# Up projections of a two-block network: high and low halves of the rows side by side in one matmul, and the bank's two halves summed by ScalarE and VectorE

## The chip, the cores and the metric

The kernel runs on one core of one Trainium2 chip. The time is that of the device, from the start of the program to its end, in microseconds (us); smaller is better. A core has a matmul engine (TensorE, PE in the profile, with its weight loads as PEld), three engines for everything else (VectorE or DVE, ScalarE or ACT, GpSimd or POOL) and a queue for loads (SyncE, SP). Each runs its own program in order, and they wait for one another by semaphores. Matmuls write to PSUM, eight banks of 128 x 512 fp32.

## What is computed

Two blocks of two layers each, on 256 rows of 1024 features. The first block has attention and a feed-forward part with a causal convolution over the rows; the second block is not touched by the change. Its part that matters here, cut:

```python
D_MODEL, SEQ, DEPTH, CONV_WIDTH = 1024, 256, 2, 3
D_FF = 2816                      # 22 tiles of 128

def conv_ffn(h, w_up, conv_w, conv_b, w_down):
    u = causal_dwconv(h @ w_up, conv_w, conv_b)   # 1024 -> 5632, three taps along the rows
    g, up = jnp.split(u, 2, axis=-1)
    return (jax.nn.silu(g) * up) @ w_down         # 2816 -> 1024

# in first_block, for both layers:
    x = x + conv_ffn(rms_norm(x, ln_ffn_g[i]), w_up[i], conv_w[i], conv_b[i], w_down[i])
```

## The kernel before

**Halves.** A matmul takes both operands in a reduced fp32 form. To keep precision each operand is split in two, a high half (the value rounded to that form) and a low half (the rest), and each product is the sum of three matmuls: high x high, high x low, low x high. Weights come by DMA as units of 128 x 1024 fp32 (512 KB) into RAW, five slots. `split` makes the high half SPH on ScalarE (L1437) and the low half SPL on VectorE (L1985), four slots; a slot is used again when TensorE has done with the unit four before it. So the halves of a unit are made at most four units ahead. The activations' halves are HTH and HTL, laid out as 8 tiles of the contraction (kt) by 512 columns; the feed-forward part uses columns 0 to 255, the 256 rows.

**The feed-forward stage.** `block1` runs it for layer 0 and 1, here FFN 0 and FFN 1. For each of 22 tiles j, TensorE does the up unit of side 0 (the gate) and of side 1, then the down unit of tile j - 2. An up unit is `turned` on half a bank: for each kt three matmuls of 256 columns (L975 high x high, L976 with the rows' low half, L977 with the weights' low half), 24 in all. Both sides of a tile share one bank, side 0 in columns 0 to 255 and side 1 in the rest. A down unit is 12 matmuls of 512 columns (L1139 to L1141) into banks 4 to 7. In FFN 0 the up banks are 0, 1 and 2; in FFN 1 they are 0 to 3.

**What follows an up tile (`up`).** When both sides are in the bank, ScalarE makes FC for both sides (L1557: last tap and bias), VectorE adds the two other taps to each side, reading the bank (L2198, L2201, twice), ScalarE takes the tanh (L1561), VectorE finishes the gated product FT (L2206, L2210), ScalarE rounds it to AH (L1568), and GpSimd subtracts to get AL (L2604). AH and AL are what the down unit needs. I call VectorE's first L2198 of a tile "the start of FC on VectorE". The bank is free after VectorE's last L2201.

**Order.** There is no scheduler at run time. `Schedule` writes one list of steps, and each engine's program takes its own share of it in that order. Whenever a weight unit is asked for (`get_w`), the splits of the next units are written into the list just there. In a tile the list reads: up of j, split, (down unit of j - 2), split, up unit of side 0 of j + 1, split, up unit of side 1, up of j + 1. Into FFN 0 are woven, in tiles 1 to 18, the matmuls of another projection (`ada`, L1040), whose weights aren't split; in tile 3 ScalarE also issues four table loads. FFN 1 has in tile 2 the norm statistics of the second block's context, in tile 3 the rope tables, in tiles 5 to 12 one context product each (`prod`: two small matmuls, VectorE, ScalarE, and VectorE or GpSimd).

## Time and profile before

| | us |
|---|---|
| median of three runs (2135.65 to 2137.37) | 2136.27 |
| span of the profiled execution | 2132.1 |
| TensorE busy in it | 2081.3 |
| VectorE busy | 1337.3 |
| ScalarE busy | 961.3 |
| GpSimd busy | 134.3 |

The profile is of one execution and its span leaves out what lies around the program, 4.2 us against the median. FFN 0 lies from about 154 to 354 us, FFN 1 from about 499 to 693. A busy time is the sum of an engine's instructions; matmuls overlap, each is listed with 0.28 or 0.39 us, while the next starts 0.12 or 0.23 us after it. So distances are read from start to start. In the timelines a row is a start, a length, the engine and the line, and at its end, where there is one, how long the engine was idle before it and who ended that.

### The profile page before, as it was taken

What the parts mean: (1) busy time and instruction counts of PE and PEld (TensorE: products, weight loads), DVE (VectorE), ACT (ScalarE), POOL (GpSimd) and SP (SyncE); (2) the same over time, 40 slices, a digit from 0 to 9 for tenths busy, and PEclk for the clock granted to TensorE, in tenths of its full rate; (3) what the DMA queues carried; (4) which work ended last, traced back from release to release, by engine and by line L of the source; (5) the groups of instructions that cost most, each with busy time, mean ns of one, the idle gap of its engine ahead of it and who ended that gap; (6) DMA issues with size and microseconds to landing.
All of it is one profiled execution on the core that took longest, in us unless ns stands there. A gap on an engine that the chain in (4) does not pass through costs nothing.

```text
span 2132.1 us, 31611 instructions
## 1 busy us (share of the span) xinstructions
PE 2081.3 (98%) x12202; PEld 1795.3 (84%) x12202; DVE 1337.3 (63%) x2333; ACT 961.3 (45%) x1602; POOL 134.3 (6%) x140
## 2 busy tenths in 40 slices
PE   8999999999999999999999999999989999999998
PEld 6779998778999888888888788888877899888997
DVE  6756667667777227548445556868563578475665
ACT  4545555554555425353333453232343554445443
POOL 1001000000110100000100001111110000100100
PEclk9999999999999999999999999999999999999999
DMA  8436655534555321222222104534224234251553
GB/s 258 144 129 239 227 209 193 162 100 166 181 178 176 126 99 60 70 70 70 79 89 89 60 30 152 197 109 158 100 100 141 89 126 140 91 178 55 193 169 129
DMA packets 79099, 284.23 MB, mean 133 GB/s; under 512 B 8790, under 2 KB 9698, under 8 KB 78952
## 3 DMA queue, kind: packets, MB, share of 16 engines
q1 hardware_dynamic: 70848, 256.15, 35.5%
q10 hardware_dynamic: 6072, 18.73, 2.4%
q0 software_dynamic: 2032, 7.35, 1.2%
q8 instruction: 98, 1.61, 0.3%
q14 instruction: 49, 0.40, 0.1%
HBM read 276.35 MB, written 5.83 MB: 132 GB/s over the span
## 4 chain that ended last, share of the span: by engine, by line
PE 80%; DVE 10%; ACT 6%; issue 2%; DMA 2%; POOL 0%; DVEq 0%; ACTq 0%; SPq 0%
PE pb L975 15%; PE pb L977 15%; PE pb L976 15%; PE pb L988 5%; PE pb L990 5%; PE pb L989 5%; DVE SPL L1985 3%; PE pb L994 2%; PE pb L1139 2%; ACT SPH L1437 2%; PE pb L1141 2%; PE pb L1140 2%; PE pb L1316 2%; PE pb L1213 2%; PE pb L1297 2%
## 5 line engine op out<-in xcount | busy, mean ns | idle before, releaser
L1985 DVE TENSOR_TENSOR SPL<-RAW,SPH 128x1024 fp32r<-128x1024 f32 x462 | 561.0, 1229 | 409.3 <-ACT SPH L1437 395.7
L975 PE MATMUL pb<-HTH,SPH 128*128 128x256 f32 (+1 forms) x2008 | 646.6, 322 | 6.8 <-DVE HTL L2063 3.0
L977 PE MATMUL pb<-HTH,SPL 128*128 128x256 f32 (+1 forms) x2008 | 637.4, 317 | 0.0
L976 PE MATMUL pb<-HTL,SPH 128*128 128x256 f32 (+1 forms) x2008 | 637.2, 317 | 0.0
L1437 ACT ACTIVATE SPH<-RAW 128x1024 fp32r<-128x1024 f32 x462 | 476.8, 1048 | 243.0 <-PE pb L977 118.9
L975 PEld LDWEIGHTS pb<-HTH,SPH 128*128 128x128 f32 x2008 | 382.2, 190 | 38.3 <-issue 4.7
L976 PEld LDWEIGHTS pb<-HTL,SPH 128*128 128x128 f32 x2008 | 382.4, 190 | 26.2
L977 PEld LDWEIGHTS pb<-HTH,SPL 128*128 128x128 f32 x2008 | 382.2, 190 | 26.0
L988 PE MATMUL pb<-SPH,HTH 128*128 128x512 f32 x640 | 254.9, 398 | 2.5 <-ACT GV L1635 2.0
L990 PE MATMUL pb<-SPL,HTH 128*128 128x512 f32 x640 | 250.6, 392 | 0.0
L989 PE MATMUL pb<-SPH,HTL 128*128 128x512 f32 x640 | 250.2, 391 | 0.0
L988 PEld LDWEIGHTS pb<-SPH,HTH 128*128 128x128 f32 x640 | 120.9, 189 | 29.7 <-issue 2.7
L990 PEld LDWEIGHTS pb<-SPL,HTH 128*128 128x128 f32 x640 | 120.6, 188 | 25.9
L989 PEld LDWEIGHTS pb<-SPH,HTL 128*128 128x128 f32 x640 | 121.1, 189 | 23.8
L975 PE MATMUL pb<-ABH,SPH 128*128 128x512 f32 (+1 forms) x384 | 131.6, 343 | 1.7 <-DVE SPL L1985 1.1
L977 PE MATMUL pb<-ABH,SPL 128*128 128x512 f32 (+1 forms) x384 | 129.8, 338 | 0.0
L976 PE MATMUL pb<-ABL,SPH 128*128 128x512 f32 (+1 forms) x384 | 129.8, 338 | 0.0
L975 PEld LDWEIGHTS pb<-ABH,SPH 128*128 128x128 f32 x384 | 72.3, 188 | 10.7 <-issue 2.2
L1798 ACT ACTIVATE GT<-pb,BG 128x512 f32<-128x512 f32 (+1 forms) x48 | 27.8, 579 | 117.9 <-PE pb L977 117.9
L977 PEld LDWEIGHTS pb<-ABH,SPL 128*128 128x128 f32 x384 | 72.2, 188 | 8.6
L976 PEld LDWEIGHTS pb<-ABL,SPH 128*128 128x128 f32 x384 | 72.3, 188 | 8.5 <-issue 0.2
L1139 PE MATMUL pb<-SPH,AH 128*128 128x512 f32 x176 | 71.3, 405 | 1.8 <-ACT SPH L1437 1.8
(274 smaller groups left out, 2503.3 us busy)
## 6 DMA issues: line engine op xcount, KB each, us to landing
RAW<-in_w_up SPq DMA_DIRECT2D x88, 512.0 KB, 4.5
RAW<-in_wa SPq DMA_DIRECT2D x64, 512.0 KB, 3.3
RAW<-in_w_in SPq DMA_DIRECT2D x48, 512.0 KB, 4.6
...
```

The costliest lines, as they stand in the source:

```text
L975: T.matmul(o, wh[:, kt, :], xh[:, kt, n0:n1], start=kt == 0, stop=False)
L976: T.matmul(o, wh[:, kt, :], xl[:, kt, n0:n1], start=False, stop=False)
L977: m = T.matmul(o, wl[:, kt, :], xh[:, kt, n0:n1], start=False, stop=kt == 7)
L988: T.matmul(P[:, :], xh[:, kt, c], wh[:, j, :], start=kt == 0, stop=False)
L989: T.matmul(P[:, :], xl[:, kt, c], wh[:, j, :], start=False, stop=False)
L990: m = T.matmul(P[:, :], xh[:, kt, c], wl[:, j, :], start=False, stop=kt == 7)
L994: return T.transpose(o, i, ident)
L1139: T.matmul(P[:, :], xh, wh, start=j == 0, stop=False)
L1140: T.matmul(P[:, :], xl, wh, start=False, stop=False)
L1141: m = T.matmul(P[:, :], xh, wl, start=False, stop=end)
L1437: A.activation(hi, raw, ACT.Copy, scale=1.0).then_inc(*act.tick(s["hi"], ("u", u)))
L1985: W.tensor_tensor(lo, raw, hi.bitcast(F32), SUB).then_inc(*dve.tick(s["lo_dve"], ("u", u)))
```

## The change

Each side of an up tile gets a bank of its own. HTH and HTL become the two parts of one array HT2, so that one matmul can stream the 256 rows' high halves and their low halves, 512 columns, past the weights' high half. The new function `paired` does this: for each kt one matmul of 512 columns over the whole bank and one of 256 with the weights' low half into the first half of the bank; for the last kt the order is reversed. The bank's first half then holds two of the three products, its second half the third. A new step `up_sum` follows each up unit: ScalarE copies the second half to the new array FU, VectorE adds the first half to it and frees the bank. `up` then reads FU and no longer the bank; ScalarE's FC of a side now waits for VectorE's sum of that side.

```diff
         for j in range(FF_TILES + 2):
             if j < FF_TILES:
-                n = self.take(LO4 if l else (0, 1, 2), ("up", l, j))
                 for side in range(2):
                     u = self.get_w(f"w_up{l}", side * FF_TILES + j)
+                    n = self.take(LO4 if l else (0, 1, 2), ("up", l, j, side))
                     self.add("up_mm", l, j, side, u)
                     self.put_w(u)
+                    self.add("up_sum", l, j, side)
+                    self.give(n)
                 self.add("up", l, j)
-                self.give(n)
...
+    def paired(P, hi, lo, src, kts=range(8)):
+
+        wh, wl = (a.rearrange("p (k c) -> p k c", k=8) for a in (hi, lo))
+        both = sb["AB2" if src[0] == "AB" and src[2] != "s" else "HT2"]
+        apart = P[:, :].rearrange("p (a n) -> p a n", a=2)
+        for kt in kts:
+            rows(src, kt)
+            xs = both[:, :, kt, 0:256]
+            if kt < 7:
+                T.matmul(apart, wh[:, kt, :], xs, start=kt == 0, stop=False)
+            m = T.matmul(apart[:, 0, :], wl[:, kt, :], both[:, 0, kt, 0:256], start=False, stop=False)
+            if kt == 7:
+                m = T.matmul(apart, wh[:, kt, :], xs, start=False, stop=True)
+        return m
...
     def up_mm(l, j, side, u):
-        P = bank(("up", l, j))
-        hi, lo = halves(u)
-        m = turned(P[:, side * 256:side * 256 + 256], hi, lo, (f"f{l}",), 0, 256)
+        P = bank(("up", l, j, side))
+        m = paired(P, *halves(u), (f"f{l}",))
...
+    def up_sum(l, j, side):
+        name = ("up", l, j, side)
+        act.wait_ge(mm, name)
...
+        A.activation(sb["FU"][:, j % 2, side, :], k.P(name)[:, 256:512], ACT.Copy, scale=1.0).then_inc(
+            *act.tick(s["ffn_act"], ("low", l, j, side)))
+
     def up(l, j):
-        P, C, i = k.P(("up", l, j)), sb["FC"], j % 2
+        C, i = sb["FC"], j % 2
         for side in range(2):
             ft = side * FF_TILES + j
-            act.wait_ge(mm, ("up", l, j, 1))
+            act.wait_ge(*k.read(("up", l, j, side)))
...
-            A.activation(C[:, i, side, :], P[:, side * 256:side * 256 + 256], ACT.Identity,
+            A.activation(C[:, i, side, :], sb["FU"][:, i, side, :], ACT.Identity,
...
+    def up_sum(l, j, side):
+        name, U = ("up", l, j, side), sb["FU"][:, j % 2, side, :]
+        dve.wait_ge(s["ffn_act"], ("low", l, j, side))
+        W.tensor_tensor(U, k.P(name)[:, 0:256], U, ADD).then_inc(*dve.free(*k.read(name)))
+
...
-            c, u = C[:, i, side, :], P[:, side * 256:(side + 1) * 256]
+            c, u = C[:, i, side, :], sb["FU"][:, i, side, :]
             dve.wait_ge(s["ffn_act"], ("c", l, j, 1))
```

What this does to the order, on VectorE in FFN 0, from the start of FC of tile 20 to that of tile 21. L1985 is a weight split; pb0 is the bank. Before:

```order
L2198 SCALAR_TENSOR_TENSOR FC_132<-pb0,PAR_55,FC_132 128x255 [waits ffn_act]
L2201 SCALAR_TENSOR_TENSOR FC_132<-pb0,PAR_55,FC_132 128x254 [waits ffn_dve]
L2198 SCALAR_TENSOR_TENSOR FC_132<-pb0,PAR_55,FC_132 128x255
L2201 SCALAR_TENSOR_TENSOR FC_132<-pb0,PAR_55,FC_132 128x254 [waits ffn_dve]
L2206 SCALAR_TENSOR_TENSOR FT_133<-FT_133,FC_132 128x256 [waits ffn_act]
L2210 SCALAR_TENSOR_TENSOR FT_133<-FT_133,FC_132 128x256 [waits read0,ffn_dve]
L1985 TENSOR_TENSOR SPL_51<-RAW_49,SPH_50 128x1024 [waits mm,hi,raw1]
L1985 TENSOR_TENSOR SPL_51<-RAW_49,SPH_50 128x1024 [waits mm,hi,raw2]
L1985 TENSOR_TENSOR SPL_51<-RAW_49,SPH_50 128x1024 [waits mm,hi,raw3]
L2198 SCALAR_TENSOR_TENSOR FC_132<-pb1,PAR_55,FC_132 128x255 [waits ffn_act]
```

The same place after; L2011 is the split, L2220 the sum, L2229 and L2232 the two taps:

```order
L2229 SCALAR_TENSOR_TENSOR FC_130<-FU_132,PAR_54,FC_130 128x255 [waits ffn_act]
L2232 SCALAR_TENSOR_TENSOR FC_130<-FU_132,PAR_54,FC_130 128x254 [waits ffn_dve]
L2229 SCALAR_TENSOR_TENSOR FC_130<-FU_132,PAR_54,FC_130 128x255
L2232 SCALAR_TENSOR_TENSOR FC_130<-FU_132,PAR_54,FC_130 128x254 [waits ffn_dve]
L2236 SCALAR_TENSOR_TENSOR FT_131<-FT_131,FC_130 128x256 [waits ffn_act]
L2240 SCALAR_TENSOR_TENSOR FT_131<-FT_131,FC_130 128x256 [waits ffn_dve]
L2011 TENSOR_TENSOR SPL_51<-RAW_49,SPH_50 128x1024 [waits mm,hi,raw1]
L2011 TENSOR_TENSOR SPL_51<-RAW_49,SPH_50 128x1024 [waits mm,hi,raw2]
L2220 TENSOR_TENSOR FU_132<-pb1,FU_132 128x256 [waits ffn_act]
L2011 TENSOR_TENSOR SPL_51<-RAW_49,SPH_50 128x1024 [waits mm,hi,raw3]
L2220 TENSOR_TENSOR FU_132<-pb2,FU_132 128x256 [waits ffn_act]
L2229 SCALAR_TENSOR_TENSOR FC_130<-FU_132,PAR_54,FC_130 128x255 [waits ffn_act]
```

A sum stands between the second and the third split, and another between the third split and FC. On ScalarE, from FC of tile 20 to that of tile 21, before (L1557 FC, L1437 the high half of a split):

```order
L1557 ACTIVATE FC_132<-pb0,PAR_55 128x256 [waits ffn_pool,ffn_act,mm]
L1557 ACTIVATE FC_132<-pb0,PAR_55 128x256
L1561 ACTIVATE FT_133<-FC_132 128x256 [waits ffn_dve]
L1568 ACTIVATE AH_134<-FT_133 128x256 [waits ffn_dve]
L1437 ACTIVATE SPH_50<-RAW_49 128x1024 [waits raw1]
L1437 ACTIVATE SPH_50<-RAW_49 128x1024 [waits mm,raw2]
L1437 ACTIVATE SPH_50<-RAW_49 128x1024 [waits mm,raw3]
L1557 ACTIVATE FC_132<-pb1,PAR_55 128x256 [waits ffn_pool,ffn_act,mm]
```

And after (L1569 is the copy of up_sum, L1583 FC, L1452 the high half); `read0` to `read2` are the signals that VectorE's sum gives when it frees that bank:

```order
L1583 ACTIVATE FC_130<-FU_132,PAR_54 128x256 [waits ffn_pool,ffn_act,read2]
L1583 ACTIVATE FC_130<-FU_132,PAR_54 128x256 [waits read0]
L1587 ACTIVATE FT_131<-FC_130 128x256 [waits ffn_dve]
L1594 ACTIVATE AH_133<-FT_131 128x256 [waits ffn_dve]
L1452 ACTIVATE SPH_50<-RAW_49 128x1024 [waits raw1]
L1452 ACTIVATE SPH_50<-RAW_49 128x1024 [waits mm,raw2]
L1569 ACTIVATE FU_132<-pb1 128x256 [waits ffn_act,mm]
L1452 ACTIVATE SPH_50<-RAW_49 128x1024 [waits raw3]
L1569 ACTIVATE FU_132<-pb2 128x256 [waits ffn_act,mm]
L1583 ACTIVATE FC_130<-FU_132,PAR_54 128x256 [waits ffn_pool,ffn_act,read1]
L1583 ACTIVATE FC_130<-FU_132,PAR_54 128x256 [waits read2]
```

FC waited for TensorE (`mm`) and now waits for a bank that VectorE frees (`read`); a copy stands ahead of the third high half, and one behind it. The pattern is the same in each tile.

## Rows read from the trace of the kernel before

**Rows 1.** The page's first section: busy time, share and instructions of each engine.
```profile
PE 2081.3 (98%) x12202; PEld 1795.3 (84%) x12202; DVE 1337.3 (63%) x2333; ACT 961.3 (45%) x1602; POOL 134.3 (6%) x140
```
**Rows 2.** Busy time by stretch, FFN 1; then granted clock, DMA share, GB/s.
```profile
core 0: us, PE busy (x) PEld busy (x) DVE busy (x) ACT busy (x) POOL busy (x), PEclk, DMA share, GB/s
640.00:680.00 40.00, 40.00 (x280) 37.42 (x280) 29.11 (x44) 20.88 (x33) 2.97 (x4) 1.00 0.60 197
```
**Rows 3.** TensorE's waits, 150 to 355 us, then 500 to 700: total, times, longest.
```profile
PE pb L975 <- DVE HTL L2063: 1.4, 1, 1.4
...
PE pb L1139 <- ACT SPH L1437: 1.8, 1, 1.8
```
**Rows 4.** VectorE's timeline in FFN 0: start, length, engine, line, idle time before.
```profile
337.90 0.48 DVE L2198 SCALAR_TENSOR_TENSOR FC<-pb,PAR,FC 128x255 f32<-128x255 f32 x1 [0.84 <-ACT FC L1557]
...
342.09 3.50 DVE L1985 TENSOR_TENSOR SPL<-RAW,SPH 128x1024 fp32r<-128x1024 f32 x3 [1.49 <-ACT SPH L1437]
346.43 0.48 DVE L2198 SCALAR_TENSOR_TENSOR FC<-pb,PAR,FC 128x255 f32<-128x255 f32 x1 [0.84 <-ACT FC L1557]
```
**Rows 5.** ScalarE's timeline, same place.
```profile
336.84 1.02 ACT L1557 ACTIVATE FC<-pb,PAR 128x256 f32<-128x256 f32 x2 [1.47 <-PE pb L977]
...
340.95 2.94 ACT L1437 ACTIVATE SPH<-RAW 128x1024 fp32r<-128x1024 f32 x3
```
**Rows 6.** VectorE's timeline, first tiles of FFN 1: the starts of FC.
```profile
506.47 0.48 DVE L2198 SCALAR_TENSOR_TENSOR FC<-pb,PAR,FC 128x255 f32<-128x255 f32 x1 [1.49 <-ACT FC L1557]
...
512.94 0.48 DVE L2198 SCALAR_TENSOR_TENSOR FC<-pb,PAR,FC 128x255 f32<-128x255 f32 x1
...
519.40 0.48 DVE L2198 SCALAR_TENSOR_TENSOR FC<-pb,PAR,FC 128x255 f32<-128x255 f32 x1
...
529.27 0.47 DVE L2198 SCALAR_TENSOR_TENSOR FC<-pb,PAR,FC 128x255 f32<-128x255 f32 x1
...
537.85 0.47 DVE L2198 SCALAR_TENSOR_TENSOR FC<-pb,PAR,FC 128x255 f32<-128x255 f32 x1
...
545.62 0.48 DVE L2198 SCALAR_TENSOR_TENSOR FC<-pb,PAR,FC 128x255 f32<-128x255 f32 x1
```
**Rows 7.** TensorE's timeline: up and down units in FFN 0; then wide matmuls elsewhere.
```profile
330.89 0.28 PE L975 MATMUL pb<-HTH,SPH 128*128 128x256 f32 x1
...
336.64 0.39 PE L1139 MATMUL pb<-SPH,AH 128*128 128x512 f32 x1
...
339.42 0.28 PE L975 MATMUL pb<-HTH,SPH 128*128 128x256 f32 x1
...
17.00 0.39 PE L989 MATMUL pb<-SPH,HTL 128*128 128x512 f32 x1
...
22.01 0.39 PE L990 MATMUL pb<-SPL,HTH 128*128 128x512 f32 x1
```
**Rows 8.** Groups by form: count, busy us, mean ns of one, idle before.
```profile
L1557 ACT ACTIVATE FC<-pb,PAR 128x256 f32<-128x256 f32 x88 | 44.8, 559 | 50.5 <-PE pb L977 50.5
...
L2429 DVE SCALAR_TENSOR_TENSOR GT<-GT,pb 128x256 f32<-128x256 f32 x16 | 6.7, 419 | 1.0
...
L1746 ACT ACTIVATE WA<-WA,PAR 128x256 f32<-128x256 f32 x8 | 4.1, 507 | 17.5 <-DVE WA L2332 17.5
```
**Rows 9.** VectorE's timeline in FFN 1: a tile with a context product, and the last tile.
```profile
554.59 0.48 DVE L2198 SCALAR_TENSOR_TENSOR FC<-pb,PAR,FC 128x255 f32<-128x255 f32 x1 [0.82 <-ACT FC L1557]
...
559.25 3.50 DVE L1985 TENSOR_TENSOR SPL<-RAW,SPH 128x1024 fp32r<-128x1024 f32 x3 [1.50 <-ACT SPH L1437]
...
685.62 0.48 DVE L2198 SCALAR_TENSOR_TENSOR FC<-pb,PAR,FC 128x255 f32<-128x255 f32 x1 [0.84 <-ACT FC L1557]
```
**Rows 10.** VectorE's timeline in FFN 0: the first tile, and the one with table loads.
```profile
161.03 0.48 DVE L2198 SCALAR_TENSOR_TENSOR FC<-pb,PAR,FC 128x255 f32<-128x255 f32 x1 [1.50 <-ACT FC L1557]
...
182.78 0.48 DVE L2198 SCALAR_TENSOR_TENSOR FC<-pb,PAR,FC 128x255 f32<-128x255 f32 x1
...
188.71 3.50 DVE L1985 TENSOR_TENSOR SPL<-RAW,SPH 128x1024 fp32r<-128x1024 f32 x3 [3.24 <-ACT SPH L1437]
```

More of the change, by code:

```diff
@@ L2713, in build @@
     o = m.put("SPL", o, [128, 4, 1024], F32R)
[L2714 to L2715 removed]
+    o = m.put("HT2", o, [128, 2, 8, 512], F32R)
     D = o
```

27 lines of the change are left out of this document (15 added, 12 removed).

## The prediction

> **What bounds the kernel now.** I read the page's first section, then busy time by stage, then the waits of TensorE, and last the timelines of the three engines around one FFN tile. TensorE is busy for 2081.3 of 2132.1 us [rows 1]. In the stretch of FFN 1 it is busy all of the time, VectorE 29.11 of 40 us and ScalarE 20.88 of 40, at granted clock 1.00 [rows 2]. Once an FFN stage is under way TensorE waits 1.8 us in FFN 1 and 1.4 us in FFN 0, once each [rows 3]. So TensorE sets the time, and the other two look as if they had a quarter or half to give. The busy share hides something, though: they form a ring. Per FFN tile (one j: two up units, one down unit) VectorE does three weight splits and six small steps, ScalarE does its share between them, and each waits for the other in program order. Take the tile whose FC work starts on VectorE at 337.90. ScalarE can't make the next high half before AH is done, at 340.95; VectorE can't make the low half before 342.09, which is 4.19 us after 337.90. Three low halves follow at (3.50 - 1.23) / 2 = 1.135 us from start to start, 3.41 us; then VectorE is idle 0.84 us until ScalarE's FC, which waited for TensorE, and starts again at 346.43 [rows 4, 5]. **The ring is 4.19 + 3.41 = 7.60 us long; TensorE's tile is 346.43 - 337.90 = 8.53 us.** That ring is real where TensorE leaves it alone: with two low halves it should be 4.19 + 2 x 1.135 = 6.46, and the starts 506.47, 512.94 and 519.40 lie 6.47 apart, the last two with no idle time before them [rows 6].
>
> **Part 1, the matmuls.** Each up unit has 24 matmuls of 256 columns; it gets 8 of 512 and 8 of 256. The columns streamed are the same, 6144. In [rows 7] 48 narrow starts take 336.64 - 330.89 = 5.75 us, 0.1198 each. Twelve wide ones take 339.42 - 336.64 = 2.78 us, 0.2317 each; elsewhere 22 wide starts take 22.01 - 17.00 = 5.01 us, 0.2277. So a merged pair saves between 0.2396 - 0.2317 = 0.008 and 0.2396 - 0.2277 = 0.012 us, eight pairs a unit, 88 units: 5.6 to 8.4 us in the kernel. I take 0.16 us a tile, 7.0 us, where TensorE stays the bound. The wide moving operand is now two blocks of 256, 16 KB apart; no row shows that form. The bounds are a gain of 8.4 and, if a wide one cost two narrow starts, none; a loss is rival C. I take the middle of the rows, since addresses are the only thing new.
>
> The Trainium skill ("TensorE: Matmul & The Clock Gate", section "Back-to-back issue gap") gives the spacing of a warm matmul as N/2.4 + 2.5 ns, 215.8 ns for 512 columns and 109.2 for 256. By that a pair would save 2.6 ns and the kernel 1.8 us; this trace has 228 to 232 and 120 ns, so the rows are used [rows 7].
>
> **Part 2, the sums.** Each up unit gets a ScalarE copy of the bank's second half (up_sum), then a VectorE addition that frees the bank. ScalarE's FC step moves behind the addition of its side. The order rows in the section on the change show where: VectorE now runs low half, low half, sum of side 0, low half, sum of side 1, FC. A 256-wide VectorE step with a bank among its inputs is 0.419 us [rows 8]. What this does to the ring, step by step:
> - Sum 0 stands between low halves: 0.42, less the 1.23 - 1.135 = 0.09 by which independent steps overlap, 0.33 us. Its ScalarE copy can start about 5 us after FC, after two high halves, while VectorE reaches the sum only at 4.19 + 2 x 1.135 = 6.46; the copy is hidden, and so is the one of side 1.
> - Sum 1 is followed by ScalarE's FC of side 1, which needs its result: 0.42 + 0.04. The 0.04 is the hand-over seen from ScalarE's FC end, 336.84 + 1.02 = 337.86, to VectorE's start at 337.90 [rows 4, 5].
> - That FC step used to lie beside VectorE's low halves, since it needed TensorE alone. Now it is in the ring: 0.56 + 0.04. The row with the bank as input has 0.559; its nearest SBUF-only kin, with a scale, has 0.507 [rows 8]. FC of side 0 is done meanwhile.
> Together 0.33 + 0.46 + 0.60 = **1.39 us, so the ring becomes 9.0 us against TensorE's 8.53 - 0.16 = 8.37.** VectorE falls 0.6 us behind a tile. It can do so only until its low halves come late: the low half made right after FC (342.09 + 1.23 = 343.3) is for the down unit that TensorE starts at 339.42 + 5.75 = 345.2 [rows 4, 7], so 1.9 us of cover, of which the later FC start takes about 0.5. The two short tiles at the start (part 3) alone use that up. From then on TensorE waits for a low half in every tile and the stage runs at the ring's pace. The matmul saving is then worth nothing there.
>
> Bounds of the 1.39: with FC at 0.507, 1.34; with nothing overlapped at sum 0 and a sum at FC's 0.48 us [rows 4], 0.42 + 0.06 + 0.06 more, 1.55. No row excludes a slightly shorter sum, so I allow 1.30; a ring shorter than before is excluded, since two steps and a wait come into it and none goes.
>
> **Part 3, FFN 1 by tiles.** Starts of FC before: 506.47, 512.94, 519.40, 529.27, 537.85, 545.62 [rows 6]; eight tiles with context products at 554.59 - 545.62 = 8.97; eight plain ones at 8.53; the last FC is at 685.62 [rows 9]. In all 179.15 us for 21 steps. After:
> - two steps with two splits, ring-bound before: 2 x (6.47 + 1.39) = 15.7
> - the step with the context statistics and the one with the rope tables, ring-bound before (9.87 and 8.58): + 1.39 each, 21.2
> - one plain step, 9.0
> - eight with a product: there VectorE's low half starts 559.25 - 554.59 = 4.66 after FC, not 4.19 [rows 9], so 9.46 each, 75.7
> - eight plain, 72.0
> Sum 193.6, which is **+14.5 us**.
>
> **Part 4, FFN 0.** 161.03 to 346.43 [rows 10, 4] is 185.4 us for 21 steps. Here TensorE also runs ada matmuls, so its tile is longer: from 182.78 to 346.43, 18 steps, 9.09 us on average, and 8.93 with the saving. The ring of 9.0 is about the same. After: two short steps 15.7; one plain 9.0; the step with the table loads, where VectorE's first low half comes 188.71 - 182.78 = 5.93 after FC [rows 10], 9.0 + 1.74 = 10.7; seventeen at 9.0, 153.0, and three more ScalarE row copies of 0.3 between them, 0.9. Sum 189.3, **+3.9 us**. The start and the end of the stages I count at nothing: the first FC comes some 0.3 later in each, the last tile's tail some 0.5 shorter, since TensorE's queue there is shorter. The three-bank ring of FFN 0 (a bank a side now, three sides deep, not three tiles) doesn't bind: sum 0 frees its bank 6.5 us after FC, TensorE wants it again after a down unit and an up unit more.
>
> **The sum.** 14.5 + 3.9 = +18.4 us on the profiled 2132.1 us. The median of the runs is 2136.3, 4.2 more for what lies around the span, which doesn't change. Forecast **2154.7 us**, 0.9% slower. About 42 steps scale with the 1.39: at 1.30 it is 3.8 us less, at 1.55 6.7 more, so 2151 to 2161; the count of steps in which TensorE is really held adds a few us either way, mostly in FFN 0, 2147 to 2165.
>
> **Rivals.**
> A, faster: the sums fit in VectorE's free time and TensorE stays the bound. For it: 27% of VectorE's time is free in [rows 2], and TensorE hardly waits now [rows 3]. It needs the three additions to stay under 8.37 - 7.60 = 0.77 us. Two 0.42 sums alone pass that, before the FC hand-over. It would give 2136.3 - 7.0 = 2129.3.
> B, no difference: the ring grows by about 1.0, to 8.6. This would happen if FC of side 1 were hidden by something I misread in the order. FFN 1 would lose 21 x (8.6 - 8.37) plus the start, some +7, FFN 0 would gain 3: about 2140.
> C, slower than forecast: a merged matmul of two blocks runs at its listed 0.39 us and not at 0.23. Then TensorE's tile is 8.37 + 16 x 0.16 = 10.9 us and becomes the bound again, 42 steps 2.2 us longer each: about 2228. From this rival's point on, 0.27 us a wide matmul, TensorE is slower than the ring. Against it: each matmul of the trace starts long before the one ahead ends, at every width [rows 7].
> D, the clock. I expect TensorE idle for 1.8 + 2 x 1.39 = 4.6 us in one piece, in FFN 1 behind the context statistics, where it waits 1.8 now [rows 3]. The granted clock is 1.00 in the stretch of rows 2, and no row here shows the other level. Should one down unit of 2.78 us behind the gap take twice as long, that is 2.8 us more, of which the ring, setting the pace, may take back some: about 2157.
> The same page of the Trainium skill (section "HAM oscillation — how this bites in real kernels") warns that idle gaps between bursts of matmuls return the clock to half rate; no row here shows it, and it gives D its place.
> E, the merging isn't one: each wide matmul is split again. The ring doesn't ask TensorE, so FFN 1 stays as it is and FFN 0 loses about 1: 2156.
>
> **Chances.** Forecast 0.74, A 0.10, B 0.06, C 0.03, D 0.05, E 0.02. A measurement of this kernel can tell about 0.2% (4.3 us) from no change. A is faster. B is around the edge, 4 in 6 counted as the same. The forecast's low tail, if FFN 0 gains and the ring is short, is the rest of "same". The range goes from 2146 to 2166, which holds the forecast, D, E, and leaves A, B and C out. Faster 0.10, same 0.05, slower 0.85.
>
> **What would show it.** Right: VectorE's FC starts 9.0 us apart in plain tiles of FFN 1 and 9.4 to 9.5 with a product; no idle time on VectorE between the sum of side 1 and FC other than ScalarE's FC, some 0.6; TensorE waiting for a low half (the split's line) at the down units, 0.6 us a tile, some 20 us in FFN 1; TensorE's busy time lower by some 7 us or more. Outside the two FFN stages every distance as before. Wrong: FC starts at 8.37 (A), TensorE waiting on a bank rather than a low half, wide matmuls starting over 0.24 us apart (C), or a granted clock under 1.00 (D).

## The result: 1.1% slower, by the ring of VectorE and ScalarE

| | before | after |
|---|---|---|
| median of the runs, us | 2135.96 (four, 2135.1 to 2137.37) | 2161.76 (four, 2158.15 to 2164.5) |
| ratio, with 95% interval | | 1.0113 (1.0102 to 1.0125) |
| span of the profiled execution | 2132.1 | 2156.3 |
| FFN 0, first to last FC start | 185.4 | 190.2 |
| from there to the first FC start of FFN 1 | 160.0 | 165.3 |
| FFN 1, first to last FC start | 179.1 | 194.6 |

The changed kernel takes 25.8 us more by the medians and 24.2 by the spans; the forecast was 18.4 more, 2154.7 us, range 2146 to 2166. The two stages are what was forecast (+4.8 for +3.9, +15.4 for +14.5). The rest lies between them, where I had counted nothing. In the spans 24.2 - 18.4 = 5.8 us are missing from the forecast: 1.8 in the stages, 5.3 between them, 0.2 ahead of the first FC, and 1.6 the other way behind the last one. The medians miss by 7.1; the other 1.3 is that after's profiled execution lies further under its kernel's median than before's. (A run's time is some 1.8 us over its span in nearly all runs that list both, so of the 4.2 put down to "what lies around the program" more than half is that this one profiled execution was short.)

The busy line of the profile after, which answers to [rows 1]:

```profile
PE 2087.4 (97%) x11498; PEld 1760.9 (82%) x11498; DVE 1367.9 (63%) x2421; ACT 992.1 (46%) x1690; POOL 135.3 (6%) x140
```

There are 704 matmuls fewer, yet TensorE is busy for 6 us more. A busy time counts a matmul ahead of a wait with its whole length, 0.39 us where the next one used to start after 0.23, and 42 such waits would make some 7 us; matmuls at half clock are listed longer still, with 0.63 us. This is an estimate, no run sets the parts apart. VectorE still looks idle for more than a third of the time and ScalarE for more than half. The stretch of [rows 2] after; at the end of a row stand granted clock, DMA share and GB/s:

```profile
640.00:680.00 40.00, 38.44 (x200) 31.95 (x199) 29.37 (x50) 24.17 (x40) 3.70 (x5) 1.00 0.52 173
```

TensorE is no longer busy all of the time, although its clock is full. VectorE's timeline of after, a plain tile in FFN 1 from FC to FC (L2229 FC, L2011 the low half, L2220 the sum; columns as in [rows 4]):

```profile
693.27 0.48 DVE L2229 SCALAR_TENSOR_TENSOR FC<-FU,PAR,FC 128x255 f32<-128x255 f32 x1 [0.67 <-ACT FC L1583]
...
697.48 2.36 DVE L2011 TENSOR_TENSOR SPL<-RAW,SPH 128x1024 fp32r<-128x1024 f32 x2 [1.49 <-ACT SPH L1452]
699.75 0.42 DVE L2220 TENSOR_TENSOR FU<-pb,FU 128x256 f32<-128x256 f32 x1
700.09 1.22 DVE L2011 TENSOR_TENSOR SPL<-RAW,SPH 128x1024 fp32r<-128x1024 f32 x1
701.22 0.42 DVE L2220 TENSOR_TENSOR FU<-pb,FU 128x256 f32<-128x256 f32 x1
702.31 0.48 DVE L2229 SCALAR_TENSOR_TENSOR FC<-FU,PAR,FC 128x255 f32<-128x255 f32 x1 [0.67 <-ACT FC L1583]
```

702.31 - 693.27 = 9.04 us, forecast 9.0. Nothing in that ring waits for TensorE any more: the two idle times are for ScalarE, 1.49 for the high half and 0.67 for FC of side 1, which is the step that had lain beside other work. ScalarE, same place:

```profile
700.21 0.60 ACT L1583 ACTIVATE FC<-FU,PAR 128x256 f32<-128x256 f32 x1 [0.38 <-DVE FU L2220]
701.67 0.60 ACT L1583 ACTIVATE FC<-FU,PAR 128x256 f32<-128x256 f32 x1 [0.86 <-DVE FU L2220]
```

And TensorE, the end of the up unit of side 1 and the down unit behind it (L990, L991 and L993 `paired`, L1154 a down unit):

```profile
698.03 0.39 PE L993 MATMUL pb<-HT,SPH 128*128 128x512 f32 x1
698.80 0.47 PE L1154 MATMUL pb<-SPH,AH 128*128 128x512 f32 x1 [0.38 <-issue]
699.11 0.39 PE L1155 MATMUL pb<-SPH,AL 128*128 128x512 f32 x1
```

The down unit starts 0.77 us after the matmul ahead of it, where 0.23 is usual. The low half that was made first in the tile starts at 697.48 and takes 1.23, so it is done at 698.71. The wait is real, but the view names no split as its cause. TensorE's waits of after, 500 to 700 us, answer to [rows 3]:

```profile
PE pb L1154 <- ACT SPH L1452: 7.4, 7, 4.3
PE pb L1154 <- issue: 3.5, 9, 0.4
PE pb L990 <- DVE HT L2089: 2.6, 1, 2.6
```

The 4.3 is the gap behind the context statistics, which the prediction put at 4.6; before it was 1.8.

### The profile page after: what moved, and what is told of

Its sections match the earlier page's. It is cut to its first block, busy times and chain, and to the rows that moved or that the text cites. A ratio compares the mean times of both kernels' runs of the same rounds, so it can differ in the third digit from the quotient of the medians.

```text
span 2156.3 us, 30371 instructions
## 1 busy us (share of the span) xinstructions
PE 2087.4 (97%) x11498; PEld 1760.9 (82%) x11498; DVE 1367.9 (63%) x2421; ACT 992.1 (46%) x1690; POOL 135.3 (6%) x140
## 3 DMA queue, kind: packets, MB, share of 16 engines
q0 software_dynamic: 2032, 7.35, 1.2%
## 4 chain that ended last, share of the span: by engine, by line
PE 70%; DVE 18%; ACT 7%; issue 3%; DMA 1%; POOL 0%; ACTq 0%; DVEq 0%
PE pb L976 11%; PE pb L978 11%; PE pb L977 11%; PE pb L1004 6%; DVE SPL L2011 6%; PE pb L1006 6%; PE pb L1005 6%; ACT SPH L1452 3%; PE pb L1010 2%; PE pb L990 2%; PE pb L1331 2%; PE pb L1228 2%; DVE FC L2232 2%; PE pb L1312 2%; DVE FC L2229 1%
## 5 line engine op out<-in xcount | busy, mean ns | idle before, releaser
L2011 DVE TENSOR_TENSOR SPL<-RAW,SPH 128x1024 fp32r<-128x1024 f32 x462 | 563.2, 1229 | 399.7 <-ACT SPH L1452 390.3
L1452 ACT ACTIVATE SPH<-RAW 128x1024 fp32r<-128x1024 f32 x462 | 478.7, 1048 | 229.3 <-PE pb L978 111.3
L976 PE MATMUL pb<-HT,SPH 128*128 128x256 f32 (+1 forms) x1304 | 447.0, 343 | 3.9 <-DVE SPL L2011 1.2
L978 PE MATMUL pb<-HT,SPL 128*128 128x256 f32 (+1 forms) x1304 | 438.2, 336 | 0.0
L977 PE MATMUL pb<-HT,SPH 128*128 128x256 f32 (+1 forms) x1304 | 438.0, 336 | 0.0
L976 PEld LDWEIGHTS pb<-HT,SPH 128*128 128x128 f32 x1304 | 247.2, 190 | 32.6 <-issue 4.7
L978 PEld LDWEIGHTS pb<-HT,SPL 128*128 128x128 f32 x1304 | 247.2, 190 | 26.0
L977 PEld LDWEIGHTS pb<-HT,SPH 128*128 128x128 f32 x1304 | 247.4, 190 | 24.8
L1004 PE MATMUL pb<-SPH,HT 128*128 128x512 f32 x640 | 254.6, 398 | 2.5 <-ACT GV L1661 2.0
L1006 PE MATMUL pb<-SPL,HT 128*128 128x512 f32 x640 | 250.1, 391 | 0.0
L1005 PE MATMUL pb<-SPH,HT 128*128 128x512 f32 x640 | 249.9, 390 | 0.0
L990 PE MATMUL pb<-HT,SPH 128*128 128x512 f32 x616 | 223.3, 401 | 4.8 <-DVE HT L2089 3.9
L991 PE MATMUL pb<-HT,SPL 128*128 128x256 f32 x704 | 184.3, 282 | 0.0
L1004 PEld LDWEIGHTS pb<-SPH,HT 128*128 128x128 f32 x640 | 120.7, 189 | 29.7 <-issue 2.7
L990 PEld LDWEIGHTS pb<-HT,SPH 128*128 128x128 f32 x616 | 117.1, 190 | 32.0 <-DVE HT L2089 4.3
L1006 PEld LDWEIGHTS pb<-SPL,HT 128*128 128x128 f32 x640 | 120.5, 188 | 25.8
L991 PEld LDWEIGHTS pb<-HT,SPL 128*128 128x128 f32 x704 | 134.2, 191 | 8.0
L1005 PEld LDWEIGHTS pb<-SPH,HT 128*128 128x128 f32 x640 | 120.7, 189 | 23.7
L976 PE MATMUL pb<-AB,SPH 128*128 128x512 f32 (+1 forms) x384 | 131.6, 343 | 1.3 <-DVE SPL L2011 0.8
L977 PE MATMUL pb<-AB,SPH 128*128 128x512 f32 (+1 forms) x384 | 129.7, 338 | 0.0
L1154 PE MATMUL pb<-SPH,AH 128*128 128x512 f32 x176 | 74.1, 421 | 19.1 <-ACT SPH L1452 12.7
```

Source lines behind the costliest of these rows:

```text
L976: T.matmul(o, wh[:, kt, :], xh[:, kt, n0:n1], start=kt == 0, stop=False)
L977: T.matmul(o, wh[:, kt, :], xl[:, kt, n0:n1], start=False, stop=False)
L978: m = T.matmul(o, wl[:, kt, :], xh[:, kt, n0:n1], start=False, stop=kt == 7)
L990: T.matmul(apart, wh[:, kt, :], xs, start=kt == 0, stop=False)
L991: m = T.matmul(apart[:, 0, :], wl[:, kt, :], both[:, 0, kt, 0:256], start=False, stop=False)
L1004: T.matmul(P[:, :], xh[:, kt, c], wh[:, j, :], start=kt == 0, stop=False)
```

## Experiments

The theory: the two sums and the FC step behind them make the ring 9.0 us long, and the ring sets the pace. The rivals: the merged matmuls cost something themselves; or any further work on VectorE would do the same, wherever it stands. For the 5.3 us between the stages the theory is half clock behind TensorE's new waits; the rival, that half clock falls at other places from one execution to the next. In all runs the ratio is to runs of the kernel before on the same chip. Below, "plain" and "product" are the distances between FC starts on VectorE in FFN 1, for tiles without and with a context product; a time for FFN 0 or FFN 1 runs from its first FC start to its last.

### The merging taken away, the sums kept

Six of the eight wide matmuls of an up unit become two narrow ones each again; the first and the last stay wide.

```diff
-            if kt < 7:
-                T.matmul(apart, wh[:, kt, :], xs, start=kt == 0, stop=False)
+            if kt == 0:
+                T.matmul(apart, wh[:, kt, :], xs, start=True, stop=False)
+            elif kt < 7:
+                T.matmul(apart[:, 0, :], wh[:, kt, :], both[:, 0, kt, 0:256], start=False, stop=False)
+                T.matmul(apart[:, 1, :], wh[:, kt, :], both[:, 1, kt, 0:256], start=False, stop=False)
```

> The changed kernel with the merging of six of the eight wide matmuls of an up unit undone (two narrow ones in its place), the sums kept; nothing left out. If the ring of VectorE and ScalarE sets the pace, TensorE's tile grows by 0.1 us, from 8.4 to 8.5 us, still under the ring's 9.04: VectorE's FC starts stay 9.04 us apart in the plain tiles of FFN 1 and 9.51 with a product, and the kernel takes 2160 to 2165 us. If the wide two-block matmul is what made the kernel slower, the spacing falls toward 8.5 and the time toward 2136.

Measured: 2158.94 us (four runs), ratio 1.0103 (1.0088 to 1.0118), overlapping with after's 1.0102 to 1.0125; the time is 1 us under what was expected, the spacing as expected. Two plain tiles at the end of FFN 1, VectorE's timeline:

```profile
675.51 0.48 DVE L2232 SCALAR_TENSOR_TENSOR FC<-FU,PAR,FC 128x255 f32<-128x255 f32 x1 [0.67 <-ACT FC L1586]
...
684.54 0.48 DVE L2232 SCALAR_TENSOR_TENSOR FC<-FU,PAR,FC 128x255 f32<-128x255 f32 x1 [0.67 <-ACT FC L1586]
```

9.03 us, as with the merging. The merged matmul neither costs nor brings anything while the ring is longer. So what the change costs doesn't lie in the matmuls.

### VectorE's sum left out

This kernel leaves VectorE's addition out: FU keeps the one product that ScalarE copied, and the other two are missing from the up projection.

```diff
-            *act.tick(s["ffn_act"], ("low", l, j, side)))
+            *act.free(*k.read(name)))
...
-        dve.wait_ge(s["ffn_act"], ("low", l, j, side))
-        W.tensor_tensor(U, k.P(name)[:, 0:256], U, ADD).then_inc(*dve.free(*k.read(name)))
+        return
```

> The changed kernel without VectorE's sum; FU holds ScalarE's copy of the bank's second half alone, so two of the three products of the up projections are left out of the result. ScalarE's copy frees the bank. Ring theory: the ring falls back to about 7.6 us, TensorE sets the pace at about 8.4 us a tile (8.8 with a product), its waits at the down units go, and the kernel takes 2129 to 2132 us, 5 to 7 below the kernel before. Clock theory (the pace is lost to a lower granted clock or to the matmuls): it stays above 2150.

Measured: 2135.06 us (ten runs), ratio 0.9990 (0.9981 to 1.0000). Plain 8.41 to 8.43, product 8.85, FFN 0 183.1, FFN 1 179.0. TensorE has the pace again, at 8.41 to 8.43 us a plain tile where the forecast of that bound was 8.37. The gain over before is under what was expected, 2129 to 2132. So even with the additions for nothing the merging is worth one or two us, no more than a measurement can tell. FFN 0 gains 2.3 us. FFN 1 gains next to nothing over before's first profile: the short first tiles stay ring-bound (6.61 us here, 6.47 before), and the step behind the context statistics is 9.37 instead of 8.59 with TensorE at half clock in it. And the stretch between the stages is 162.5 us instead of 160.0 (more on both below).

### One more step in the ring

Here the ring gets a step more: VectorE copies the bank's first half once to a spare array, ahead of the sum of side 1.

```diff
+        if side:
+            W.tensor_scalar(sb["FX"][:, :], k.P(name)[:, 0:256], 1.0, None, MUL).then_inc(*dve.tick(s["ffn_dve"]))
```

> The changed kernel with one more VectorE step in the ring: before the sum of side 1 the bank's first half is copied to an unused array. Nothing is left out. Ring theory: FC spacing grows by the pace of such a step, 0.34 to 0.46 us, in every ring-bound tile, 9.04 to 9.4-9.5, about 40 tiles, so the kernel takes 2175 to 2182 us. If TensorE's clock or its matmuls set the pace, VectorE has a quarter of its time free and it stays within 3 us of 2162.

Measured: 2175.86 us (four runs), ratio 1.0189 (1.0172 to 1.0206). Two FC starts near the end of FFN 1:

```profile
672.88 0.48 DVE L2231 SCALAR_TENSOR_TENSOR FC<-FU,PAR,FC 128x255 f32<-128x255 f32 x1 [0.67 <-ACT FC L1583]
...
682.24 0.48 DVE L2231 SCALAR_TENSOR_TENSOR FC<-FU,PAR,FC 128x255 f32<-128x255 f32 x1 [0.67 <-ACT FC L1583]
```

9.36 us for 9.04, and 0.32 to 0.34 more in 39 of the 42 steps (0.45, 0.22 and 0.17 in the other three). FFN 0 and FFN 1 are each 6.9 us longer than after's. Every tenth of a us put into this ring costs about 4 us of the kernel. Together with the run without the sum (ring shorter, pace 8.41 to 8.43) this settles what sets the pace.

### The same work, in another place

VectorE alone: the third split, which stood between the two sums, moves behind the second one. Nothing is taken away.

```diff
+    steps, held = [], None
+    for step in sched.steps:
+        if step[0] == "up_sum" and step[3] == 0:
+            held = []
+        elif step[0] == "split" and held is not None:
+            held.append(step)
+            continue
+        steps.append(step)
+        if step[0] == "up_sum" and step[3] == 1:
+            steps += held
+            held = None
```

> The changed kernel with one thing moved on VectorE alone: the low half that stood between the two sums of a tile comes after the second sum, so it runs beside ScalarE's FC. Nothing is left out. Ring theory: the ring is 4.19 + 2 x 1.135 + 0.33 + 0.33 + 1.135 = 8.26 us instead of 9.04, under TensorE's 8.4; FC starts 8.4 apart in plain tiles, 8.8 with a product; 2130 to 2138 us. If the mere time of the two sums on VectorE were the cost and not their place, it would stay within 3 us of 2162.

Measured: 2140.37 us (ten runs), ratio 1.0015 (1.0005 to 1.0024). VectorE's timeline in FFN 0, one tile:

```profile
219.97 0.48 DVE L2229 SCALAR_TENSOR_TENSOR FC<-FU,PAR,FC 128x255 f32<-128x255 f32 x1
...
224.16 2.36 DVE L2011 TENSOR_TENSOR SPL<-RAW,SPH 128x1024 fp32r<-128x1024 f32 x2 [1.49 <-ACT SPH L1452]
226.44 0.42 DVE L2220 TENSOR_TENSOR FU<-pb,FU 128x256 f32<-128x256 f32 x1
227.67 0.42 DVE L2220 TENSOR_TENSOR FU<-pb,FU 128x256 f32<-128x256 f32 x1 [0.81 <-ACT FU L1569]
228.01 1.22 DVE L2011 TENSOR_TENSOR SPL<-RAW,SPH 128x1024 fp32r<-128x1024 f32 x1
229.15 0.48 DVE L2229 SCALAR_TENSOR_TENSOR FC<-FU,PAR,FC 128x255 f32<-128x255 f32 x1
```

The median is 2 us over the 2130 to 2138 that were expected, though the ring does what was expected. ScalarE's FC of side 1 now lies beside the split at 228.01, and VectorE goes from that split to FC without idle time. Where the ring alone sets the pace it is 8.27 us; in plain tiles of FFN 1 TensorE sets it, 8.41 to 8.43. FFN 0 is 183.8, FFN 1 180.6. Some 20 of the 24 us are gone with both sums still made. The ring is 0.67 us over the 7.60 of before, which is the sums, and 0.77 under after's 9.04, which is FC waiting behind them with nothing beside it. In plain tiles the 0.67 costs nothing, as it stays under TensorE's own 8.41. What stays over before's FFN 1 is in the first tiles: 7.14 instead of 6.47 twice, 10.54 instead of 9.87 behind the context statistics, and the two steps after it, 9.30 and 8.40 instead of 8.59 and 7.76, with half clock as in before's second profile (9.33 and 8.53).

### The sum given to GpSimd

ScalarE copies the whole bank, GpSimd adds the halves, VectorE does nothing more than before.

```diff
-        A.activation(sb["FU"][:, j % 2, side, :], k.P(name)[:, 256:512], ACT.Copy, scale=1.0).then_inc(
-            *act.tick(s["ffn_act"], ("low", l, j, side)))
+        A.activation(sb["FU"][:, j % 2, side, :], k.P(name)[:, :], ACT.Copy, scale=1.0).then_inc(
+            *act.free(*k.read(name)))
...
+    def up_sum(l, j, side):
+        U = sb["FU"][:, j % 2, side, :]
+        pool.wait_ge(*k.read(("up", l, j, side)))
+        G.tensor_tensor(U[:, 0:256], U[:, 0:256], U[:, 256:512], ADD).then_inc(
+            *pool.tick(s["ffn_pool"], ("sum", l, j, side)))
```

> The changed kernel with the sum on GpSimd: ScalarE copies the whole bank (512 wide, about 0.59 us) to FU and frees it, GpSimd adds the two halves in SBUF, about 0.75 us. Nothing is left out. Ring theory: VectorE's ring is 7.6 us again, but FC comes some 2.3 us after TensorE's up unit instead of 1.75, so the low half for the down unit has only 0.3 us of cover; 2130 to 2142 us. If any sum in the chain costs what it did, above 2155.

Measured: 2181.43 us (four runs), ratio 1.0206 (1.0189 to 1.0223), the slowest of all, and a clear miss. The view of the instructions that touch FU has count, then shortest, median and longest in ns; then rows of the timeline of GpSimd, VectorE and ScalarE in one tile:

```profile
L2629 POOL TENSOR_TENSOR FU<-FU x88: 732/1562/3662, 161.7 to 734.3; 128x256 f32<-128x256 f32 x88
```

```profile
721.86 4.04 DVE L2011 TENSOR_TENSOR SPL<-RAW,SPH 128x1024 fp32r<-128x1024 f32 x3 [1.49 <-ACT SPH L1452]
...
723.27 3.23 POOL L2629 TENSOR_TENSOR FU<-FU 128x256 f32<-128x256 f32 x2 [1.64 <-ACT FU L1569]
...
726.53 0.60 ACT L1583 ACTIVATE FC<-FU,PAR 128x256 f32<-128x256 f32 x1 [1.08 <-POOL FU L2629]
...
727.17 0.48 DVE L2228 SCALAR_TENSOR_TENSOR FC<-FU,PAR,FC 128x255 f32<-128x255 f32 x1 [1.27 <-ACT FC L1583]
```

The addition takes 0.73 us when VectorE is idle and 1.56 in the median, since both fall on VectorE's splits; and the three splits take 4.04 us instead of 3.50 [rows 4]. ScalarE's FC waits for GpSimd, VectorE waits 1.27 for FC, and the plain tile is 9.51 us. My expectation took the 0.74 of AL, which GpSimd makes while VectorE waits, as the price of any such step. The Trainium skill ("SBUF — State Buffer", section "SBUF: two separate sides") states that a VectorE step with two SBUF inputs and a GpSimd step that reads SBUF share a pair of ports, which one of them holds for its whole instruction. A split has two such inputs, and the traces agree: the five additions of 88 that meet no VectorE step take 0.73 to 0.75 us, and in a tile near the end the second addition starts at 658.18, 1.12 us ahead of the end of the split beside it, and takes 1.72.

### ScalarE's first high half earlier

In each tile VectorE waits 1.49 us for a high half, which ScalarE makes only behind AH. Here it makes it behind FC and ahead of the tanh.

```diff
+        if early is not None:
+            split(early)
...
+    steps = list(sched.steps)
+    for n, step in enumerate(sched.steps):
+        if step[0] != "up":
+            continue
+        for m in range(n + 1, len(steps)):
+            if steps[m][0] in ("split", "up_sum", "up", "res2"):
+                break
+        if steps[m][0] == "split":
+            steps[n], steps[m] = step + (steps[m][1],), ("none",)
```

> The changed kernel with one step moved on ScalarE alone: the first high half after a tile's FC is made before the tanh, in ScalarE's wait for VectorE, and not after AH. Nothing is left out. Ring theory: VectorE's first low half no longer waits for AH; the ring is about 4.15 + 1.135 + 0.33 + 1.135 + 0.46 + 0.64 = 7.85 us, under TensorE's 8.41; FC starts 8.4 apart in FFN 1's plain tiles, 6.4 to 6.6 in the first two, FFN 1 from first to last FC 177 to 179 us. In FFN 0 the weights may not have landed by then, and the tanh would wait behind them: some tiles over 9.2. In all 2131 to 2140 us.

Measured: 2142.29 us (nine runs), ratio 1.0025 (1.0014 to 1.0036), 2 us over the upper end of what was expected. FFN 1 is 179.6, with ring-bound plain tiles at 8.00 and short ones at 6.70. FFN 0 is 183.1, but uneven, 8.00 to 10.85 us a tile behind the first: ScalarE waits there for down weights that haven't landed, 13.4 us in seven waits. Both stages together are 1.9 us under before's, so the second way out of the ring is worth as much there as the first. What makes the kernel slower than before lies between them, 169.7 us instead of 160.0. At the end of FFN 0 ScalarE waits 3.39 us for the next unit's weights with the tanh of the last tile behind it, TensorE waits 3.45 us for AL, and the last down matmul starts 11.7 us after the last FC, not 6.9. Both at once, the moved split in both stages and the early high half in FFN 1 only:

> The changed kernel with both moves: on VectorE the low half behind both sums, in both FFN stages; on ScalarE the high half before the tanh, in FFN 1 only. Nothing is left out. The ring would be about 7.1 us in FFN 1 and 8.3 in FFN 0, TensorE sets the pace: FFN 1 from first to last FC 176 to 178 us, FFN 0 about 184; 2130 to 2136 us, 2 to 7 below the kernel before.

Measured: 2138.27 us (ten runs), ratio 1.0006 (0.9997 to 1.0016), 2 us over the upper end of what was expected. FFN 0 183.7, FFN 1 178.8, plain 8.40 to 8.43, product 8.85. In the stages it is 1.6 and 0.4 us under before's first profile, but the median isn't lower: the stretch between them is 166.2 us, 5 to 6 more than in the two profiles of the kernel before (below). With the ring out of the way the change is worth nothing that can be measured.

### The early high half without the change

The kernel before, with the early high half in FFN 1 and nothing of the change.

> The kernel before with one thing moved, in FFN 1 alone: ScalarE makes the first high half of a tile behind FC and ahead of the tanh, not behind AH. None of the change is in it. Ring theory: VectorE's low half no longer waits 1.5 us for a high half, so where the ring set the pace (steps of 6.47, 9.87 and 8.58 us in the first tiles) they come closer, 1 to 3 us in all; the plain tiles stay at 8.53, since TensorE sets their pace. FFN 1 176 to 178 us instead of 179.15, time 0.0 to 0.15% under before's, 2133 to 2136 against 2136 to 2137. Rival (each us out of the ring is worth something everywhere): plain tiles below 8.5 us and over 5 us gained.

Measured: 2136.24 us (eleven runs), 0.2 over what was expected, ratio 0.9992 (0.9983 to 1.0001). FFN 1 takes 177.8 us instead of 179.1, all of it from the two short tiles, 5.76 instead of 6.47 [rows 6]; plain tiles stay at 8.53. That is less time in FFN 1 than with the merging and both moves (178.8, in part by half clock behind the context statistics, where a step is 9.36 instead of 8.59). So no version here beats the kernel before by more than a measurement can tell.

### Dummy matmuls against half clock

Matmuls of the identity with itself in an otherwise idle bank, 14 ahead of the first up unit of a stage and 12 ahead of the last down unit (a fp32 one counts as two in the rows), to keep TensorE at work in its waits.

```diff
+                    if j == 0 and side == 0:
+                        self.add("warm", n, 14)
...
+                if j == FF_TILES + 1:
+                    self.add("warm_late", ("up", l, FF_TILES - 1, 1), 12)
```

> The changed kernel with matmuls added that compute nothing, in TensorE's idle stretches at the two ends of the FFN stages: 14 of 128 columns before the first up unit, 12 before the last down unit. Clock theory for the part of the slowdown that the ring doesn't explain (5.3 us between the FC of the last tile of FFN 0 and that of the first tile of FFN 1, with granted clock 0.88 and 0.83 there): the clock stays at 1.00 in these places, FC of tile 21 of FFN 0 to FC of tile 0 of FFN 1 falls from 165.3 to 160 to 162 us, and the kernel takes 2155 to 2158 us; the ring's spacing stays 9.04. If those 5 us are waits and not the clock, the added matmuls change nothing or cost 1 to 3 us.

Measured: 2165.66 us (four runs), ratio 1.0139 (1.0124 to 1.0154), a miss. TensorE's timeline, last down unit of FFN 0 and entry of FFN 1:

```profile
359.32 2.84 PE L1044 MATMUL pb<-IDENT 128*128 128x128 f32 x24
361.92 0.48 PE L1163 MATMUL pb<-SPH,AH 128*128 128x512 f32 x1
...
363.16 0.40 PE L1165 MATMUL pb<-SPL,AH 128*128 128x512 f32 x1
363.40 0.40 PE L1163 MATMUL pb<-SPH,AH 128*128 128x512 f32 x1
...
513.15 3.39 PE L1039 MATMUL pb<-IDENT 128*128 128x128 f32 x28 [1.29 <-DVE HT L2098]
516.30 0.47 PE L994 MATMUL pb<-HT,SPH 128*128 128x512 f32 x1
```

The down unit runs at 0.23 us a matmul here, so its half clock (below) is gone, and its last matmul starts 7.4 us after the last FC start instead of 8.3. But the dummies at the entry stood behind the wait for the rows' halves, not in it: they start when that wait ends and hold the up unit back by 516.30 - 513.15 = 3.15 us. FFN 0 has the same 3.39 us of dummies. The first FC there comes at 167.01, against 161.26 and 163.25 in the two profiles of after. At the end of FFN 1, where after has full clock (below), the dummies cost 0.6 us, 7.37 instead of 6.75. The delays are more than the half clock had cost. What the run tells is the 0.9 us at the tail of FFN 0; for the rest it was badly built.

### Both kernels profiled a second time

> The kernel before, unchanged, profiled a second time, with a look at the stretch between the two stages: from the FC start of tile 21 of FFN 0 to that of tile 0 of FFN 1 on VectorE. Before's first profile has 160.04 us there, after's 165.33. Theory 1 (the change makes the 5.3 us there: TensorE, held up by the ring at the end of FFN 0 and at the entry of FFN 1, meets half clock): this profile again has 160.0 to 160.3, and FFN 0 185.4, FFN 1 179.1 us. Rival (where the half clock falls differs from one execution to the next, and before's first profile was a lucky one in this stretch): this one has 162 or more there, or some us more in another stretch, with the same median time of 2135 to 2138.

> The kernel after, unchanged, profiled a second time. Theory 1: 165.0 to 165.6 us between the stages again, TensorE at half pace behind the down unit of tile 21 and behind the entry of FFN 1, FFN 0 190.2, FFN 1 194.6. Rival: the half clock lies elsewhere, and this stretch has another length, between 160 and 165, while the two stages still have 190.2 and 194.6, since there the ring sets the pace.

Measured: before again 2136.57 us (ten runs), ratio 0.9995 (0.9986 to 1.0005), span 2135.8; after again 2159.74 us (one run), span 2157.9. The stretch between the stages, cut at the start of the last wide matmul of the down unit of tile 21 and at the start of the first up unit:

| | before | before again | after | after again |
|---|---|---|---|---|
| last FC start to last down matmul | 6.88 | 6.88 | 8.29 | 8.27 |
| attention, to the first up matmul | 145.8 | 147.1 | 146.8 | 148.5 |
| first up matmul to first FC start | 7.35 | 7.35 | 10.25 | 7.73 |
| together | 160.0 | 161.3 | 165.3 | 164.5 |

The same stretch in other runs, each profiled once. In the last one nothing is changed ahead of FFN 1, so up to there it is a third profile of the kernel before:

| | no sum | split moved | high half early | both moves | before, high half early |
|---|---|---|---|---|---|
| last FC start to last down matmul | 6.75 | 6.77 | 11.68 | 6.75 | 6.88 |
| attention, to the first up matmul | 148.1 | 149.4 | 149.0 | 150.1 | 148.7 |
| first up matmul to first FC start | 7.60 | 9.37 | 9.00 | 9.31 | 7.36 |
| together | 162.5 | 165.6 | 169.7 | 166.2 | 162.9 |

Stretches of TensorE's clock, columns as in [rows 2] (a granted clock of 1.00 is 2.4 GHz, and 0.50, half clock, is 1.2; what lies between is a stretch with both): first of after, then of after again, then of before again.

```profile
355.00:360.00 5.00, 4.46 (x12) 3.31 (x12) 1.23 (x1) 1.06 (x1) 0.39 (x1) 0.66 0.01 3
...
505.00:510.00 5.00, 3.48 (x11) 3.00 (x12) 4.17 (x8) 2.48 (x6) 0.00 (x0) 0.59 0.81 272
```

```profile
470.00:475.00 5.00, 4.61 (x19) 3.62 (x18) 1.47 (x6) 3.56 (x10) 0.00 (x0) 0.59 0.33 105
...
505.00:510.00 5.00, 3.56 (x32) 3.37 (x31) 3.90 (x7) 5.00 (x10) 0.00 (x0) 1.00 0.97 361
```

```profile
465.00:470.00 5.00, 4.56 (x18) 3.81 (x17) 2.56 (x7) 2.31 (x6) 0.00 (x0) 0.66 0.09 36
...
530.00:535.00 5.00, 4.61 (x14) 3.73 (x15) 4.89 (x9) 0.95 (x3) 0.00 (x0) 0.66 0.64 198
```

Both theories hold a part. **The tail is the change's own.** In both profiles of after TensorE waits 1.8 us for AL of tile 21 and then runs most of the last down unit at half clock. TensorE's timeline of after again, with the wait and matmuls behind it:

```profile
355.27 0.40 PE L1156 MATMUL pb<-SPL,AH 128*128 128x512 f32 x1
357.47 0.47 PE L1154 MATMUL pb<-SPH,AH 128*128 128x512 f32 x1 [1.80 <-POOL AL L2634]
...
358.64 0.63 PE L1155 MATMUL pb<-SPH,AL 128*128 128x512 f32 x1
359.07 0.63 PE L1156 MATMUL pb<-SPL,AH 128*128 128x512 f32 x1
...
361.63 0.42 PE L1156 MATMUL pb<-SPL,AH 128*128 128x512 f32 x1
```

Wide matmuls start 0.43 us apart, 0.23 at full clock. No profile of the kernel before has wait or half clock there. The other runs bear this out: the six profiles with an idle wait of 1.8 us or more in this place (after, after again, merging undone, GpSimd's sum, longer ring, high half early) all have half clock there, the six without one (0.45 us at most) never. But the end of FFN 1 in after has a wait as long, and TensorE comes back at full clock:

```profile
715.45 0.47 PE L1154 MATMUL pb<-SPH,AH 128*128 128x512 f32 x1 [1.80 <-ACT SPH L1452]
...
718.09 0.39 PE L1156 MATMUL pb<-SPL,AH 128*128 128x512 f32 x1
```

It is the same in after again. There the last down matmul starts 6.75 us after the last FC start, not later than before's 6.88. So the wait by itself costs nothing, and the 1.4 us at the end of FFN 0 are the half clock. The length of a wait alone doesn't decide whether half clock follows: in the runs with the longer ring and with GpSimd's sum the wait at the end of FFN 1 is 2.1 and 2.3 us, with full clock behind it. **The entry is 0.4 us of the change for certain** (7.73 against 7.35); the other 2.5 are half clock, in one execution of the two. With half clock it is also 9.0 to 9.5 us in five other profiles of kernels with the change, and at full clock 7.6 and 7.8 in two; none of the three of the kernel before has half clock there. The wait ahead of it was 2.0 to 3.3 us in the six with half clock and 1.3 to 1.6 in the six without. So the change may well bring this half clock more often; three profiles of the kernel before are too few to show it. **The attention varies from execution to execution of the same kernel**: 145.8, 147.1 and 148.7 us in three profiles of the kernel before, with half clock between 465 and 475 in the two longer ones, 146.8 and 148.5 in those of after, and the change alters no instruction there. After's 1.0 to 1.4 us over its counterpart are within that spread, so they aren't shown to be the change's; the cause of the spread stays open.

In the stages both profiles of after agree, 190.1 to 190.2 and 194.6 us. Those of before agree in FFN 0, 185.4, but FFN 1 has 179.1 and 180.7, with the stretch at 530 in the second. The wait ahead of it is the same in both, only the clock behind it isn't; first before, then before again:

```profile
527.18 0.47 PE L1139 MATMUL pb<-SPH,AH 128*128 128x512 f32 x1 [1.76 <-ACT SPH L1437]
```

```profile
530.39 0.57 PE L1139 MATMUL pb<-SPH,AH 128*128 128x512 f32 x1 [1.76 <-ACT SPH L1437]
```

The first goes on at 0.23 us a wide matmul, the second at 0.43, and its two next steps are 1.5 us longer together. After has half clock in the same place (below) in both, and pays nothing for it.

## Why the prediction came out as it did

- **The ring before, 7.60 against 8.53, and which of them sets the pace**: right. Leaving VectorE's additions out gives TensorE's pace back (8.41 to 8.43), and moving one split brings the ring down to 8.27.
- **The ring's growth of 1.39**: right, 9.04 for 9.0. The sum of side 1 takes 0.418. The one term off is FC from SBUF: 0.602 in the mean of 88, forecast 0.56 by the row that reads the bank, and not the 0.507 of its SBUF kin [rows 8]. That is nearly all of the 0.05 by which the ring is over the 8.99 of the sum. The row of FC, from the groups by form:

```profile
L1583 ACT ACTIVATE FC<-FU,PAR 128x256 f32<-128x256 f32 x88 | 53.0, 602 | 53.6 <-DVE FU L2220 53.6
```

- **Steps of both stages**: short tiles 7.90 (forecast 7.86), behind the table loads 10.56 (10.7), context statistics 11.28 (11.26), rope 10.02 (9.97), product 9.51 (9.46). The 42 steps times 0.04 make 1.7 us, which with the woven steps of FFN 0 is about the 1.8 that both stages are over the forecast.
- **The matmuls**: the size was too large, the sign right. A pair takes 352 ns from start to start instead of 359, so 7 to 8 ns are saved, where I took 8 to 12; TensorE's own tile is 8.41 to 8.43 and not 8.37. It didn't matter, as the run without the merging shows. "TensorE's busy time lower by some 7 us" was wrong: it rose by 6.1, for the reason told above: a wait's first 0.16 us counts as busy, and half clock does.
- **The start and the end of the stages, counted at nothing**: this is the step that failed, and it makes 5.3 of the 5.8 us that are missing in the spans. Of the 5.3 us 1.4 are the half clock behind the wait for AL, 0.4 the longer way to the first FC (forecast 0.3), 1.0 the attention, which varies more than that in the kernel before, and 2.5 half clock that this one execution had at the entry. Rival D had half clock at one place only, where it costs nothing. That the time still fell into the range is owed to the range's width, which was meant for the ring, and not to a term of the sum. I had put the tail of a stage as shorter, since TensorE's queue is shorter when it runs behind the ring. At the end of FFN 1 it is 0.1 shorter. At the end of FFN 0 that same short queue leaves TensorE with nothing to do while AL of the last tile is made, and half clock follows. Behind the last FC of FFN 1 after is 1.6 us shorter than before, but before again is 1.0 shorter too.
- **The waits' names**: I looked for waits on the split's line. The view lists ScalarE's high half and "issue" instead. The 0.5 us a tile are seen only from start to start. "0.6 us a tile, some 20 us in FFN 1" also didn't agree with itself: 21 times 0.6 is 13 us, and the view lists 7.4 + 3.5 = 10.9 at the down units.
- **Rival A** falls, by the spacing and by the 1.39 us. **B**: the ring grew by 1.4, not by 1.0. **C** falls: wide matmuls of `paired` start 0.234 us apart. **E** falls too: the trace has 704 matmuls fewer, one for each of the eight pairs of 88 units, and each wide one is a single row. **D** is real as an event: the granted clock behind the context statistics. First after, then after again, whose second row is at the lower of the two levels throughout:

```profile
535.00:540.00 5.00, 1.05 (x7) 0.64 (x5) 4.31 (x15) 4.69 (x8) 1.19 (x1) 1.00 0.02 7
540.00:545.00 5.00, 4.65 (x15) 3.76 (x16) 4.29 (x8) 1.46 (x4) 0.00 (x0) 0.66 0.66 215
```

```profile
535.00:540.00 5.00, 2.19 (x13) 1.63 (x11) 4.24 (x17) 3.71 (x8) 1.19 (x1) 0.92 0.19 77
540.00:545.00 5.00, 3.53 (x8) 2.84 (x9) 4.33 (x8) 2.47 (x5) 0.00 (x0) 0.50 0.50 136
```

TensorE did 1.05 us of work in five, and came back at half clock. The step is 11.28 and 11.29 us, the forecast without any half clock 11.26. The ring sets the pace, so a slower TensorE costs nothing in this place. This is what "the ring may take back some" came to: all of it. The Trainium skill ("TensorE: Matmul & The Clock Gate", section "HAM oscillation — how this bites in real kernels") warns of idle gaps between bursts; these rows agree with it, 4.3 us idle and half clock behind it. The waits of 1.76 and 1.80 us above were followed by half clock in one place or execution and by full clock in another.
